# Two-layer kernel: layer one projected from the raw split input, recurrent and merge stages in one block

## The chip, the cores and the metric

One core of a Trainium2 chip runs one launch. The metric is the device time of the launch in microseconds (us). The engines are named TensorE (PE), VectorE (DVE), ScalarE (ACT), GpSimd (POOL) and SyncE (SP, which issues DMAs).

## The reference, cut to what matters

Two transformer layers over 512 tokens of width 1024 (16 meta tokens are put in front in layer one, so 528).

```python
# layer one
u = rmsnorm(h, norm_mix_pre); proj = u @ w_in         # q_na k_na v_na q_gl k_gl v_gl g_gl z_gl
o = concat(rmsnorm(neighbourhood_attention(...)), gla_bidirectional(...))
h = h + rmsnorm(o @ w_o, norm_mix_post)
h = h + rmsnorm((gelu(gate) * val) @ w_ffn_out, norm_ffn_post)   # gate, val: convolved h @ w_ffn_in
# layer two
proj = rms_norm(x, norm_mix) @ w_in
attn = windowed_gqa(q, k, v, sink)                    # 512 wide
rw = rwkv7_time_mix(zr, ...)                          # recurrent branch, 512 wide
merged = gates[0] * (attn @ w_up_attn) + gates[1] * (rw @ w_up_rwkv)
x = x + merged @ w_out
x = x + square(relu(rms_norm(x) @ w_ff1)) @ w_ff2
x = x + (p @ w_ple) * sigmoid(rms_norm(x) @ w_ple_gate)
```

The norm multiplies each token by a scalar: `(h * gain * rs) @ w` equals `((h * gain) @ w) * rs`, with `rs` one number per token.

## The kernel before

**Products.** Every large product is done in three passes (`three_pass`, L238): weights and input are each split into a high part (fp32r, written by ACT) and a low part (the rest, written by DVE), and hi·hi, lo·hi and hi·lo are summed in PSUM. Weights come in slots of 128 x 2048 through a ring of two places (`Ring`, L152). For each slot SP loads `raw` (L205), ACT writes `hi` (`hi_slot`, L215), DVE writes `lo` and raises `split` (`lo_slot`, L228), and PE raises `tile_done` per tile and waits for `tile_free` before it reuses a bank. Each engine works through its own list in order.

**Opening of the mixer (`mixer_block`).** SP loads h in four pieces, then the narrow slot (32 columns of z) and the two slots of `fm_gla` (L511 to L516). ACT squares h tile by tile (L292), PE sums the squares with a matrix of ones (L300), ACT takes the root (L884), DVE the reciprocal over all 528 tokens (L1078). DVE then writes `h * gain * rs` (L1084), ACT its high part `u_hi` (L889), DVE its low part `u_lo` (L1090). PE starts the first tiles (narrow slot and slot 1) k by k after `u_done`, then slot 2 (`fm_gla`'s second), which goes into the ring place that the narrow slot held. ACT evicts these tiles (L891, L898). The token-major slots (`tm_gla`, L589 to L593) follow. POOL issues 64 small loads of the bias rows from the beginning (L550).

**GLA stage.** While PE works through the gated recurrence (decays, scores, outputs for t = 0 to 4), the products of `fm_na` and `tm_na` are dealt into PE's order in counted portions (`run(name)`), 24 matmuls to a tile, two banks in turn. ACT evicts them in `evacuate` (L931 to L937) after its exponentials; DVE splits the next slot in `split_more`. The scores of the neighbourhood attention are scaled by 0.125 on DVE (L1254).

**Recurrent stage (`rwkv_block`).** Eight units (u = 0 to 7) with five levels each. Then the state loop: for 7 chunks and two directions, DVE multiplies by a decay (L2769), PE makes products (L2483), DVE adds them (L2767). Then y for four token tiles (PE L2498, DVE L2778 to L2786, ACT squares L2598), the normalisation (L2788, L2791), and for four fi: PE transposes and gate product (L2510, L2512), ACT scale (L2605), DVE bonus and gate (L2794, L2797, `rw_t`).

**Merge stage (`merge_block`).** It has its own block: the semaphores are cleared and all engines meet (L3161, L3162), the ring's weights are loaded anew. ACT and DVE split `attn_t` and `rw_t` (L2955, L3027), PE makes 16 tiles of the up-projection, 12 matmuls of 512 columns each: eight for the attention half, eight for the recurrent half. Per tile ACT opens a gate (sigmoid, L2962), DVE multiplies (L3037), and in the second half adds the two (L3040), ACT and DVE split the sum (L2965, L3048). Then come `w_out`, four groups of `w_ff1` and `w_ff2`, and the last gate.

## Time and profile before

| | us |
|---|---|
| median of 3 runs (1850.02 to 1853.32) | 1852.45 |
| the profiled execution | 1852.69 |
| its span in the profile | 1850.9 |
| mean granted clock of TensorE | 0.974 of full |

| engine | busy us | share of the span |
|---|---|---|
| PE (matmul) | 1729.4 | 93% |
| DVE | 1018.9 | 55% |
| ACT | 650.9 | 35% |
| POOL | 88.4 | 5% |

Rows of a timeline begin with start and duration; what ended an engine's idle time stands in brackets with the idle time. Granted clock 1.00 is 2.4 GHz, 0.50 is 1.2 GHz. A matmul on fp32 (not fp32r) data is recorded as two instructions.

### The profile page before, as it was taken

Reading aid. Unit: us, or ns where it says so; the run is one execution under the profiler, and the core shown is the slowest. Engines: PE = TensorE matmul, PEld = TensorE weight load, DVE = VectorE, ACT = ScalarE, POOL = GpSimd, SP = SyncE. Lnnn points to the kernel's source line nnn. Section 1 sums busy time; section 2 is a strip of 40 time slices with the busy share of each in tenths; the row PEclk is TensorE's granted clock in tenths of the full one; section 3 lists DMA queues with packets and bytes.
Section 4 is the critical chain, followed back from the end, with each engine's and each line's share of the span. In section 5 each row is a group of like instructions: output and inputs, shape, how many; then the busy total and the mean of one; then the engine's idle time right before and its main releaser. Section 6 shows DMA issues by size and latency. Waiting matters only on the chain. (4 is left out here: it accounts for less than half of the span.)

```text
span 1850.9 us, 38611 instructions
## 1 busy us (share of the span) xinstructions
PE 1729.4 (93%) x17168; PEld 1504.6 (81%) x17168; DVE 1018.9 (55%) x1527; ACT 650.9 (35%) x1067; POOL 88.4 (5%) x115
## 2 busy tenths in 40 slices
PE   6999999889999999899999988888499999999998
PEld 5899978889989989797777777777287888888887
DVE  3237776456726636538664465564656535353565
ACT  3243335434424323433443333332334312121332
POOL 7000000100000000100000000000002000000020
PEclk9999999989999999899999999999799999999999
DMA  5211120311232222222222100000142222222221
GB/s 169 92 69 46 70 94 10 109 53 69 91 114 92 92 91 92 98 81 80 92 100 77 41 4 4 4 4 10 66 180 87 99 104 92 93 99 105 91 92 68
DMA packets 29132, 144.57 MB, mean 78 GB/s; under 512 B 6315, under 2 KB 9659, under 8 KB 14380
## 3 DMA queue, kind: packets, MB, share of 16 engines
q1 hardware_dynamic: 24828, 133.58, 20.0%
q0 software_dynamic: 3856, 7.87, 1.5%
q8 instruction: 132, 2.16, 0.5%
q10 hardware_dynamic: 288, 0.73, 0.1%
q14 instruction: 28, 0.23, 0.0%
HBM read 134.82 MB, written 8.91 MB: 78 GB/s over the span
## 5 line engine op out<-in xcount | busy, mean ns | idle before, releaser
L228 DVE TENSOR_TENSOR w_w_lo<-w_w_raw,w_w_hi 128x2048 fp32r<-128x2048 f32 x66 | 151.2, 2291 | 178.5 <-ACT w_w_hi L215 178.1
L240 PE MATMUL f_bank<-u_hi,w_w_hi 128*128 128x258 f32 x704 | 202.4, 287 | 5.0 <-DVE u_lo L1486 4.2
L241 PE MATMUL f_bank<-u_hi,w_w_lo 128*128 128x258 f32 x704 | 201.3, 286 | 0.0
L242 PE MATMUL f_bank<-u_lo,w_w_hi 128*128 128x258 f32 x704 | 199.9, 284 | 0.0
L240 PE MATMUL g_bank<-g_y_hi,g_w_hi 128*128 128x512 f32 x384 | 151.1, 393 | 12.2 <-DVE g_w_lo L228 12.1
L241 PE MATMUL g_bank<-g_y_hi,g_w_lo 128*128 128x512 f32 x384 | 150.4, 392 | 0.0
L242 PE MATMUL g_bank<-g_y_lo,g_w_hi 128*128 128x512 f32 x384 | 150.4, 392 | 0.0
L215 ACT ACTIVATE g_w_hi<-g_w_raw 128x2048 fp32r<-128x2048 f32 x45 | 85.9, 1909 | 163.5 <-PE g_bank L242 161.9
L240 PEld LDWEIGHTS f_bank<-u_hi,w_w_hi 128*128 128x128 f32 x704 | 134.1, 191 | 5.6 <-issue 4.7
L215 ACT ACTIVATE w_w_hi<-w_w_raw 128x2048 fp32r<-128x2048 f32 x66 | 125.8, 1905 | 30.9 <-PE f_bank L242 30.9
L228 DVE TENSOR_TENSOR g_w_lo<-g_w_raw,g_w_hi 128x2048 fp32r<-128x2048 f32 x45 | 108.3, 2408 | 49.6 <-ACT g_w_hi L215 49.6
L242 PEld LDWEIGHTS f_bank<-u_lo,w_w_hi 128*128 128x128 f32 x704 | 135.1, 192 | 0.0
L241 PEld LDWEIGHTS f_bank<-u_hi,w_w_lo 128*128 128x128 f32 x704 | 134.5, 191 | 0.1
L240 PE MATMUL g_bank<-g_u_hi,g_w_hi 128*128 128x512 f32 x320 | 125.4, 392 | 2.6 <-DVE g_u_lo L3048 2.6
L241 PE MATMUL g_bank<-g_u_hi,g_w_lo 128*128 128x512 f32 x320 | 125.2, 391 | 0.0
L242 PE MATMUL g_bank<-g_u_lo,g_w_hi 128*128 128x512 f32 x320 | 125.0, 391 | 0.0
L1727 PE MATMUL a_bank<-u_hi,w_w_hi 128*128 128x512 f32 x240 | 98.6, 411 | 2.3 <-DVE shift L2047 1.6
L1731 PE MATMUL a_bank<-u_lo,w_w_hi 128*128 128x512 f32 x240 | 97.8, 407 | 0.0
L1729 PE MATMUL a_bank<-u_hi,w_w_lo 128*128 128x512 f32 x240 | 97.7, 407 | 0.0
L240 PEld LDWEIGHTS g_bank<-g_y_hi,g_w_hi 128*128 128x128 f32 x384 | 72.7, 189 | 28.5 <-issue 13.4
L242 PEld LDWEIGHTS g_bank<-g_y_lo,g_w_hi 128*128 128x128 f32 x384 | 72.7, 189 | 15.4
L241 PEld LDWEIGHTS g_bank<-g_y_hi,g_w_lo 128*128 128x128 f32 x384 | 72.8, 190 | 15.0
(510 smaller groups left out, 3904.6 us busy)
## 6 DMA issues: line engine op xcount, KB each, us to landing
g_w_raw<-in_w_ff SPq DMA_DIRECT2D x32, 1024.0 KB, 4.8
w_w_raw<-in_w_in SPq DMA_DIRECT2D x30, 1024.0 KB, 4.8
w_w_raw<-in_w_ffn_in SPq DMA_DIRECT2D x22, 1024.0 KB, 4.8
w_w_raw<-in_w_ffn_out SPq DMA_DIRECT2D x12, 1024.0 KB, 4.8
w_w_raw<-in_w_o SPq DMA_DIRECT2D x4, 1024.0 KB, 5.0
gate_pre<-rw_t POOLq DMA_DIRECT2D x16, 256.0 KB, 2.3
g_w_raw<-in_w_up SPq DMA_DIRECT2D x4, 1024.0 KB, 8.8
g_branch<-gate_pre SPq DMA_DIRECT2D x4, 1024.0 KB, 11.8
```

The source lines that it names most:

```text
L215: nc.scalar.activation(R.hi[:, r, 0:size], R.raw[:, r, 0:size], ACT.Copy).then_inc(R.hi_done, 1)
L228: nc.vector.tensor_tensor(R.lo[:, r, 0:size], R.raw[:, r, 0:size], R.hi[:, r, 0:size].bitcast(F32), ALU.subtract).then_inc(R.split, 1)
L240: nc.tensor.matmul(out, w_hi, u_hi, start=start, stop=False)
L241: nc.tensor.matmul(out, w_lo, u_hi, start=False, stop=False)
L242: return nc.tensor.matmul(out, w_hi, u_lo, start=False, stop=stop)
L1727: nc.tensor.matmul(tile_bank(g), w_hi, u_hi[:, k, :], start=k == 0, stop=False)
L1729: nc.tensor.matmul(tile_bank(g), w_lo, u_hi[:, k, :], start=False, stop=False)
L1731: last = nc.tensor.matmul(tile_bank(g), w_hi, u_lo[:, k, :], start=False, stop=k == KT - 1)
```

## The change

**Layer one.** The projection takes `h * gain` without the token's scalar. ACT writes its high part straight from h, DVE its low part, and slot 1 is loaded and split in two halves (`PART`), the narrow slot gets a place of its own. Squares go on alongside and are added by DVE; PE sums them after k = 4 into one column per token tile, and after k = 6 spreads the reciprocal roots to a row (`rms`). The scalar is applied at eviction: by DVE as a product with `rms` for the feature-major tiles (now also the first eight tiles of `fm_na`, which are the keys, loaded first), by ACT's scale for the token-major ones, and for the queries in the attention scores (`rs_query`). POOL's 64 bias loads wait for the narrow tile.

**Layer two.** The recurrent and merge stages share one block; POOL clears the attention stage's semaphores during the third unit and after it. The merge stage's buffers are placed over dead ones (`Merge`). During the last unit ACT and DVE split `attn_t` and slot 0 of `w_up`. PE's attention half of the up-projection (96 matmuls) is dealt into the state loop (12), before y of the last tile (7), after it (50), and into the loop over fi (0, 6, 3, 18). ACT copies those tiles out, POOL splits slots 1 and 2 and multiplies the attention half by its gates, ACT and DVE split `rw_t` per fi. Gates are loaded after y. The merge stage keeps only slots 2 and 3.

```diff
+            sp.dma_start(R.raw[:, 1, 0:PART], w[4, :, 0:PART]).then_inc(part_loaded, 16)
+            load_h(0)
             sp.dma_start(narrow(R.raw[:, 0, :]), narrow(w[12, :, :])).then_inc(R.loaded[0], 16)
-            load_phase(sp, R, fm_gla, w[4:6])
+            load_h(1)
+            sp.dma_start(R.raw[:, 1, PART:2 * PART], w[4, :, PART:2 * PART]).then_inc(R.loaded[1], 16)
+            load_h(2)
+            load_h(3)
+            sp.wait_ge(R.split, 1)
+            sp.dma_start(R.raw[:, 0, :], w[5, :, :]).then_inc(R.loaded[0], 16)
-            load_phase(sp, R, fm_na, w[0:4])
+            load_phase(sp, R, fm_na, w[0:4], at=(2, 3, 0, 1))
...
+            pool.wait_ge(R.tile_done, zz.end())
...
+                if k == 4:
+                    pe.wait_ge(const_loaded, 16)
+                    pe.wait_ge(added, KT - 1)
+                    for t in range(5):
+                        last = nc.tensor.matmul(bank[0:size[t], 6, t:t + 1], sq_all[:, tok[t]], C("ones")[:, 0:1], start=True, stop=True)
...
+            scaled_hi(1)
+            scaled_hi(2)
+            act.wait_ge(R.loaded[1], 16)
+            nc.scalar.activation(R.hi[:, 1, PART:2 * PART], R.raw[:, 1, PART:2 * PART], ACT.Copy).then_inc(R.hi_done, 1)
+            square(0)
+            square(1)
+            for k in range(3, KT):
+                scaled_hi(k)
+                square(k - 1)
+            square(KT - 1)
...
+            for k in range(3, KT):
+                scaled_lo(k)
+                add_square(k - 1)
+            add_square(KT - 1)
...
+                    dve.wait_ge(R.tile_done, fm_gla.c0 + 2 * j + m + 1)
+                    nc.vector.tensor_tensor(gla_in[:, 2 * j + m, :].rearrange("p (a b) -> p a b", a=2), bank[:, b:b + 2, 0:HALF], row,
+                                            ALU.mult).then_inc(R.tile_free, 1)
...
+        @block.gpsimd
+        def _(pool):
+            def low(n):
+                pool.wait_ge(M.R.hi_done, n + 1)
+                nc.gpsimd.tensor_tensor(M.R.lo[:, n % 2, :], M.R.raw[:, n % 2, :], M.R.hi[:, n % 2, :].bitcast(F32), ALU.subtract).then_inc(M.R.split, 1)
+
+            pool.wait_ge(d_done, NU)
+            low(1)
+            low(2)
+            for t in range(KT):
+                pool.wait_ge(M.R.tile_free, t + 1)
+                pool.wait_ge(M.gate_open_a, t + 1)
+                nc.gpsimd.tensor_tensor(M.branch[:, t, :], M.branch[:, t, :], M.gate[:, t, :], ALU.mult).then_inc(M.gated, 1)
...
                     last.then_inc(step_done, 1)
+                    run_attn(1)
...
+                if t == 3:
+                    run_attn(7)
...
                 last.then_inc(y_done, 1)
+            run_attn(50)
...
                 nc.tensor.matmul(bank[:, fi % 2, :], lora_g[:, fi * P:fi * P + P], zr[:, 13, :], start=True, stop=True).then_inc(gl_done, 1)
+                run_attn((0, 6, 3, 18)[fi])
...
+            act.wait_ge(rp_read, NU)
+            hi_slot(act, nc, M.R, 0, 1, None)
+            keep_attn(0)
...
+            keep_attn(3)
+            hi_slot(act, nc, M.R, 1, 0, 4)
+            keep_attn(4)
...
+                if fi == 0:
+                    keep_attn(5)
+                else:
+                    split_branch(fi - 1)
+                open_gate(fi)
...
-            each_slot(dve, up, up_slot)
+            dve.wait_ge(R.split, 3)
+            for j in (2, 3):
+                up_slot(j, 1, j % 2)
...
-        nc.clear_and_free_semaphores(nc.allocated_since(before))
-        nc.all_engine_barrier()
...
-        merge_block(nc, io, C, PV, h, attn_t, rw_t, gate_pre)
+            merge_block(nc, io, C, PV, h, M, w.sem["rw_done"], block)
```

## Rows read from the trace of the kernel before

**Rows 1.** The page, busy time of TensorE.

```profile
PE 1729.4 (93%) x17168; PEld 1504.6 (81%) x17168; DVE 1018.9 (55%) x1527; ACT 650.9 (35%) x1067; POOL 88.4 (5%) x115
```

**Rows 2.** Stretches: us, busy PE, PEld, DVE, ACT, POOL (instructions), clock, DMA, GB/s.

```profile
3.00:4.50 1.50, 0.00 (x0) 0.00 (x0) 0.00 (x0) 0.00 (x0) 1.50 (x4) 1.00 0.96 383
...
18.90:27.70 8.80, 0.00 (x0) 0.00 (x0) 7.76 (x6) 4.00 (x5) 8.80 (x18) 0.78 0.74 173
...
30.40:44.00 13.60, 13.60 (x113) 13.15 (x113) 6.83 (x11) 2.71 (x5) 4.51 (x9) 0.99 0.20 49
```

**Rows 3.** Timeline of PE in the opening.

```profile
27.77 0.40 PE L240 MATMUL m_bank<-u_hi,w_w_hi 128*32 128x264 f32 x1 [8.89 <-DVE u_lo L1090]
...
50.05 0.39 PE L240 MATMUL m_bank<-u_hi,w_w_hi 128*128 128x264 f32 x1 [3.37 <-DVE w_w_lo L228]
...
64.25 0.36 PE L589 MATMUL m_bank<-w_w_hi,u_hi 128*128 128x256 f32 x1 [0.79 <-ACT m_gla_in L898]
```

**Rows 4.** Timeline of DVE and ACT in the opening.

```profile
19.86 3.45 DVE L1078 RECIPROCAL m_work<-m_work 128x528 f32<-128x528 f32 x1 [1.42 <-ACT m_work L884]
...
24.16 0.64 ACT L889 ACTIVATE u_hi<-m_work 128x528 fp32r<-128x528 f32 x1 [2.52 <-DVE m_work L1084]
...
26.92 0.70 DVE L1090 TENSOR_TENSOR u_lo<-m_work,u_hi 128x528 fp32r<-128x528 f32 x1
...
45.77 1.90 ACT L215 ACTIVATE w_w_hi<-w_w_raw 128x2048 fp32r<-128x2048 f32 x1
```

**Rows 5.** The tile h in the opening: time from issue to landing.

```profile
DMA to landing us min/median/max: 5.6/8.2/10.1
```

**Rows 6.** Timeline of ACT and DVE in the GLA stage, t = 1.

```profile
145.61 0.60 ACT L949 ACTIVATE m_work<-m_bank 128x512 f32<-128x512 f32 x1 [2.35 <-PE m_bank L663]
...
147.64 0.41 ACT L932 ACTIVATE acc<-m_bank 128x256 f32<-128x256 f32 x1
...
150.91 2.29 DVE L228 TENSOR_TENSOR w_w_lo<-w_w_raw,w_w_hi 128x2048 fp32r<-128x2048 f32 x1 [1.45 <-ACT w_w_hi L215]
```

**Rows 7.** Stretches of the tail and of the feed-forward part.

```profile
1312.00:1320.00 8.00, 0.00 (x0) 0.00 (x0) 5.55 (x12) 2.77 (x4) 0.00 (x0) 0.50 0.00 0
...
1333.00:1342.40 9.40, 0.00 (x0) 0.00 (x0) 6.79 (x3) 7.44 (x4) 0.00 (x0) 0.58 0.85 336
...
1400.00:1600.00 200.00, 200.00 (x896) 166.01 (x895) 99.15 (x98) 54.97 (x53) 13.75 (x7) 1.00 0.28 99
```

**Rows 8.** Timelines of DVE, PE and ACT in the tail.

```profile
1292.30 0.42 DVE L2769 TENSOR_TENSOR r_s<-r_s,small 128x256 f32<-128x256 f32 x1
...
1294.45 1.48 PE L2483 MATMUL r_bank<-r_s,r_gi 64*64 64x64 f32 x32 [0.19 <-DVE r_s L2769]
...
1319.64 2.50 DVE L2791 TENSOR_TENSOR zr<-zr,r_stat 128x512 f32<-128x512 f32 x4
...
1331.05 0.69 DVE L2797 TENSOR_TENSOR rw_t<-r_bank,acc 128x512 f32<-128x512 f32 x1
...
1342.50 1.28 ACT L2962 ACT_TABLE_LOAD   x1
1343.80 2.19 ACT L2962 ACTIVATE g_branch<-g_branch 128x512 f32<-128x512 f32 x4
...
1371.43 0.68 DVE L3037 TENSOR_TENSOR g_branch<-g_bank,g_branch 128x512 f32<-128x512 f32 x1
```

**Rows 9.** Chain of waits where the output projection starts: start, us, what.

```profile
1395.86 0.75 PE g_bank L240
1396.61 0.43 PE g_bank L241
```

**Rows 10.** Timelines of DVE and POOL where both work.

```profile
1418.75 3.38 DVE L228 TENSOR_TENSOR g_w_lo<-g_w_raw,g_w_hi 128x2048 fp32r<-128x2048 f32 x1
...
1418.65 4.64 POOL L310 TENSOR_TENSOR g_rows<-g_rows,g_branch 128x512 f32<-128x512 f32 x2 [6.93 <-ACT g_branch L2932]
...
747.93 1.09 POOL L310 TENSOR_TENSOR f_a<-f_a,f_c 128x512 f32<-128x512 f32 x1
```

More of the change, by code:

```diff
@@ L596, in token_tile @@
                     yield
+            pe.wait_ge(row_steps, TURNED)
+            for c in range(NB):
+                last = nc.tensor.matmul(bank[:, 6, 128 + c:129 + c], by_column[:, P * c:P * c + P], eye[:, 0:1], start=True, stop=True)
+            last.then_inc(row_steps, 1)
             def raw(t):
@@ L2198, in __init__, with __getitem__ @@
         self.half_w0, self.half_a0 = small[:, at:at + 2 * RW_FI], small[:, at + 2 * RW_FI:at + 4 * RW_FI]
-def rwkv_block(nc, io, C, PV, w, block, before):
+class Halves:
+    def __init__(self, first, second):
+        self.parts = (first, second)
+    def __getitem__(self, key):
+        rows, i, cols = key
+        half = (i.start if isinstance(i, slice) else i) // KT
+        i = slice(i.start - KT * half, i.stop - KT * half) if isinstance(i, slice) else i - KT * half
+        return self.parts[half][rows, i, cols]
```

485 lines of the change are left out of this document (343 added, 142 removed).

## The prediction

> **What bounds the kernel now.** I read the page's busy times first, then tables of stretches, then the timelines of the two places that the diff touches. TensorE (PE) is busy 93% of the span [rows 1], so an edit pays where PE stands still or runs at half clock. PE has two such places here.
>
> The opening: PE runs the norm's sums early, does nothing from 18.9 to 27.7 us, restarts at half clock, and then turns out a projection matmul of 264 columns every 0.120 us (13.60 us for 113) [rows 2]. The first starts at 27.77, released by the scaled and split activations; slot 2 starts at 50.05 after 3.37 us of waiting for its low half; the token-major slots start at 64.25, 0.79 us after an eviction by ACT [rows 3]. Behind 27.77 stands a serial chain: squares, sums, root, a 3.45 us reciprocal, scaling, splitting [rows 4].
>
> The tail: PE has no instruction from 1312 to 1320 (clock at 1.2 GHz, 0.50) and from 1333 to 1342.4, while the feed-forward part is full at 0.223 us a matmul of 512 columns (200 us for 896) [rows 7]. The last rw_t is written at 1331.05 to 1331.74, two semaphore and load steps follow, and the up-projection's 192 matmuls all come after that [rows 8]. The chain of waits enters the output projection at 1395.86 at half clock (0.75 for the first) [rows 9].
>
> **Opening, part by part.** Removed from PE's path: the 16 norm sums, root, reciprocal over 528 columns, normalising pass, and slot 2's dependence on the narrow slot's place. Added before PE: half a slot split (ACT 0.95, DVE 1.15, half of 1.90 and 2.29 [rows 4, 6]), one scaled copy (0.64) and one low half (0.70) [rows 4]. The loads are reordered; the POOL's 64 bias loads go behind the first tile. The first pieces: half of w4 (0.5 MB), h0 (0.54 MB) and params. DMA gives 383 GB/s when loaded [rows 2]; h landed 5.6 us after issue at best, 10.1 at worst [rows 5]. Half a slot ahead of h0 adds 0.5 MB / 383 GB/s = 1.4 us, less what consts takes now: h0 at about 7.2. Then the 0.64 and 0.70 and their waits make u 0 at 8.8, with weights split by 8.1. PE starts at 8.8.
>
> From there the DVE sets the pace: up to the second half slot, landing at about 11.2 and split at 13.4, it has little to do; then five pairs of low half and addition, 1.35 each, and two single additions: sum of squares ready at 21.5. PE has then done five of eight k (18 matmuls each, 2.16: 8.8 to 19.6 at full clock, 21 if it starts at half), waits to 21.5, and has three k (6.5), five sums and five spreads left (1.2 together): 29.2. Root, small reciprocals and diagonals (about 2.3 after the sums) lie under k = 5 and 6. Slot 2 is loaded by 17, split by 26.8, its bank freed by a DVE product of 0.7 to 0.8 under k = 7. Its 96 matmuls take 11.7: 40.9; one eviction by DVE, four small query sums in parallel, 0.8: token-major slots start at 41.7 in place of 64.25, **minus 22.5**. Ends: minus 24 (PE begins at 8, full clock) and minus 18 (h2 and h3 land 4 us later than 14).
>
> **Evictions moved to DVE.** Eight key half-tiles go from ACT to DVE inside the GLA stage, where PE is full. In step t = 1 ACT evicts a tile at 147.64, but DVE finishes its own products only at 149.46 (150.91 less 1.45). PE takes up the fill at 145.6, when ACT is released, and after 26 matmuls of 0.115, at 148.6, needs that bank: 24 matmuls make a tile, and there are two banks [rows 6]. The DVE then evicts in 0.6, in the 1.45 us it idles before the weight split [rows 6]: PE loses 1.4 here and 1.0 by the same reckoning in t = 2: **plus 2.4**; 0 if ACT's exponentials shift, 4 if t = 0 joins. Scales by a column in place of a constant: nothing, same instructions.
>
> **Tail, part by part.** All in the old times.
> (a) Unit 7 takes eight half-microsecond ACT pieces and eight DVE pieces of 0.6 into idle time of over 2 us a level: 0.
> (b) The state loop has a period of 1.67 us, DVE's four operations of 0.42, and PE waits only 0.19 of it [rows 8]. Two fill matmuls of 0.22 do not fit: (2 x 0.22 - 0.19) x 6 = **plus 1.6** (0 to 2.8, all twelve).
> (c) POOL now splits slot 1 as soon as ACT's high half is done, about 1292.2, just when DVE multiplies states (both inputs in SBUF). Where the two meet in the trace, a DVE split of 2.29 took 3.38, and two POOL additions of 1.09 took 4.64 [rows 6, 10]: they exclude each other for an instruction's length. POOL at 1.09 per 512 columns needs at least 4.4 for 2048. **Plus 4.4** (0 if the operation falls between, 5.2).
> (d) The y stage is DVE's; PE fills there, so it keeps its clock. From yn at 1322.14 [rows 8], ACT gets between its four scalings one kept tile, a table load of 1.28, four sigmoids at 0.55 [rows 8] and three splits: it becomes the limit. Step by step: rw_t 3 at 1333.9 and its split at 1335.1, **2.2 later** than now. POOL's second split and its first four gate products meet bonus and low-half operations of DVE: **plus 2.5** (0 to 4.8, four products of 1.2).
> (e) PE's last 18 fill matmuls end at 1335.6. The eight recurrent tiles take 96 x 0.227 = 21.8: 1357.4. The barrier, the attention half, four loads and the first weight split are gone from the path.
> (f) DVE then has multiply, add, low half per tile (0.7 + 0.6 + 0.6 [rows 8]), plus two weight splits of 2.3, and ends at 1362.6; three matmuls of the last k close output tile 0 at 1363.3. Now it ends at 1395.86 + 6 x 0.43 = 1398.4.
> Sum of the tail: 1363.3 + 1.6 + 4.4 + 2.5 = 1371.8, so **minus 26.6**. Ends: minus 35.1 (none of the pluses) and minus 20 (all upper ends, and 1.2 for POOL under slot 3's split).
>
> On the trace's 3.38 for 2.29: the Trainium skill, SBUF — State Buffer, section "Who interferes with whom", says that a DVE instruction with two SBUF inputs and a GpSimd instruction that reads SBUF cannot run together, and the later one waits for the whole of the other. The trace agrees [rows 10]; by the rule the tail has its 6.9 us of (c) and (d), and if the two engines shared instead it would have none of them, which is rival 1.
>
> **Sum.** Against the profiled execution's 1852.69 (span 1850.9, 1.8 around it; the median of the runs, 1852.45, is the same within 0.02%): 1852.7 - 22.5 + 2.4 - 26.6 = **1806.0**.
>
> **Rivals.**
> 1. *POOL and DVE miss each other*: POOL works when DVE reads PSUM (adds, y sums). Against it: half the state loop's DVE time reads SBUF twice [rows 8]. 1806.0 - 6.9 = 1799.1.
> 2. *The loads set the opening*: h3, last in the queue, lands 4 us later; DMA stands at 383 GB/s in the early stretch [rows 2], and the whole of 4 MB must pass. For it: h0 alone took 5.6. Against: the bias loads are out of the way. 1806.0 + 4.5 = 1810.5.
> 3. *The fill is not hidden*: PE has its attention matmuls in order before work that the recurrence needs; if all 96 (21.8 us) lie on the path in place of 1.6, 1806.0 + 20.2 = 1826.2. Against: PE stood idle or at half clock from 1312 to 1320 [rows 7].
> 4. *Slower than before*: POOL's split of slot 1. PE's fill tile 4 waits for it ahead of the gate transposes, at about 1316; begun at 1292, it has 24 us. Beyond, each microsecond counts in full, and 24 + 46.7 = 71 us for 2048 columns (18 us per 512) is where the change begins to lose; at 80 us it gives 1862. The rows show 1.09 to 2.8 per 512 columns, so this would need a different kind of operation.
> 5. *The change doesn't do it*: something (a wait on the cleared semaphores in unit 7, a gate load) holds the merge stage to its old start, and only the opening is won: 1852.7 - 20.1 = 1832.6.
>
> **How the numbers follow.** Forecast case 61% (1800 to 1812 on its own terms), rival 1 15%, rival 2 11%, rival 3 5%, rival 4 4% (a quarter of it near its turning point), rival 5 4%. The range 1794 to 1819 runs from all lower ends (1852.7 - 24 - 35.1 = 1793.6) to all upper ends (1852.7 - 18 + 4 - 20 = 1818.7), and leaves out rivals 3 to 5, 13%, and some of the forecast case's tails. A measurement of this kernel can tell about 0.2%, 3.7 us. Faster by more 96%, within it 1%, slower 3%.
>
> **What would show it.** Right: PE's first matmul near 9 us with a wait of some 2 us before the sums; the first token-major matmul near 42; a DVE state product of 4 to 5 us beside a POOL operation of as much; PE filled from 1290 to 1322 (old times); recurrent tiles starting 13.5 us after yn; GLA 2 us longer. Wrong: a POOL split that takes 8 us or more, state products untouched, PE waiting at the second half slot, or a DVE chain after the last recurrent tile of over 5 us.

## The result, and the profile after

| | before | after |
|---|---|---|
| median, us | 1852.88 (4 runs, 1850.02 to 1854.08) | 1822.49 (4 runs, 1816.23 to 1830.32) |
| profiled execution / its span, us | 1852.69 / 1850.9 | 1830.32 / 1828.5 |
| ratio, 95% interval | | 0.9843, 0.9817 to 0.9869 |

The change makes the kernel 30 us faster; 47 were forecast. The forecast was 1806.0 us, its range 1794 to 1819: the time lies outside. The profiled execution is the slowest of the four, 7.8 us above their median, so what is laid out below accounts for a gain of 22.4 us and not of 30. Two executions that had a mean granted clock of 0.84, one of an experiment (1931.87 us) and one of the kernel before (1966.58 us), are left out of the comparisons.

Where the two profiles part is found by laying DVE's instructions, which are nearly the same in both, side by side. Offset is after less before, at the same instruction:

| DVE instruction | before | after | offset | my sum there |
|---|---|---|---|---|
| weight split L228, start of the token-major slots | 65.94 | 47.13 | -18.8 | -22.5 |
| copy to m_state, inside the GLA stage | 168.91 | 153.04 | -15.9 | -20.1 |
| copy to the selector, start of the units | 1058.72 | 1043.39 | -15.3 | -20.1 |
| first sum behind unit 7 | 1287.80 | 1275.71 | -12.1 | -20.1 |
| first addition behind the state loop | 1303.51 | 1305.68 | +2.2 | -14.1 |
| last rw_t | 1331.05 | 1337.22 | +6.2 | -9.4 |
| first addition of the output projection | 1404.58 | 1373.21 | -31.4 | -46.7 |
| last product but one of the kernel | 1845.68 | 1823.31 | -22.4 | -46.7 |

Four places take back what was forecast: the opening (3.7 us), the units (3.2), the state loop (14.3 in place of 6.0) and, largest and not in the forecast at all, the feed-forward part (9.0). The step that replaces the merge stage's start by dealt fill gave 37.6 us (6.2 + 31.4) where the sum has 37.3.

Page of the changed kernel: busy times, and the granted clock in tenths over 40 slices.

```profile
PE 1738.0 (95%) x17164; PEld 1502.6 (82%) x17164; DVE 1023.2 (56%) x1546; ACT 653.7 (36%) x1073; POOL 110.7 (6%) x125
...
PEclk9999999989999999899999999999799999999999
...
q8 instruction: 132, 2.16, 0.5%
```

PE is busier than before [rows 1], in a shorter span: fewer holes, but slower matmuls. The 7 in the clock row is the state loop. The queue of instructions (packets, MB, share) comes up again in the units.

Timeline of ACT and PE in the opening of the changed kernel:

```profile
8.46 0.73 ACT L916 ACTIVATE u_hi<-h,params 128x528 fp32r<-128x528 f32 x1 [1.61 <-DMA h<-in_h]
...
10.14 0.56 PE L240 MATMUL m_bank<-u_hi,w_w_hi 128*128 128x264 f32 x1 [10.14 <-DVE u_lo L1132]
...
15.12 0.42 PE L241 MATMUL m_bank<-u_hi,w_w_lo 128*128 128x264 f32 x1
15.34 0.34 PE L242 MATMUL m_bank<-u_lo,w_w_hi 128*128 128x264 f32 x1
15.52 0.28 PE L240 MATMUL m_bank<-u_hi,w_w_hi 128*128 128x264 f32 x1
...
44.13 0.95 PE L627 MATMUL m_bank<-consts,m_work 128*128 128x1 f32 x8
45.44 0.36 PE L616 MATMUL m_bank<-w_w_hi,u_hi 128*128 128x256 f32 x1 [0.36 <-ACT m_st L950]
```

ACT's first scaled copy waits for the first piece of h, which was issued at 1.20 and landed 7.2 us later. PE starts at 10.14 in place of 27.77 [rows 3], runs its first matmuls 0.22 us apart, that is at half clock, until 15.3, then 0.12 apart, and never waits before 45.

Stretches around the state loop, changed kernel (us, busy PE, PEld, DVE, ACT, POOL with instructions, clock, DMA share, GB/s), and the loop's stretch of the kernel before:

```profile
1266.00:1279.40 13.40, 9.30 (x367) 8.32 (x358) 7.66 (x15) 5.21 (x9) 0.00 (x0) 1.00 0.23 82
1279.40:1292.00 12.60, 9.72 (x97) 6.64 (x96) 7.34 (x12) 0.60 (x1) 4.51 (x1) 0.59 0.24 85
1292.00:1305.00 13.00, 12.73 (x148) 9.25 (x149) 5.46 (x13) 0.60 (x1) 0.00 (x0) 0.50 0.00 1
```

```profile
1287.00:1303.00 16.00, 11.92 (x378) 10.20 (x371) 12.25 (x29) 0.60 (x1) 0.00 (x0) 1.00 0.01 3
```

The same loop ran at 1.00 before and runs at 0.50 to 0.59 now. Its timeline in the changed kernel (PE, POOL and DVE; L3058 is the addition that closes each half step, L3060 the state product):

```profile
1278.80 0.35 PE L2694 MATMUL r_bank<-r_s,r_gi 64*64 64x64 f32 x5 [1.26 <-DVE r_s L3060]
1280.14 4.51 POOL L2456 TENSOR_TENSOR g_lo<-g_raw,g_hi 128x2048 fp32r<-128x2048 f32 x1 [236.91 <-ACT g_hi L215]
1280.76 0.56 PE L2694 MATMUL r_bank<-r_s,r_gi 64*64 64x64 f32 x11 [1.60 <-issue]
1281.36 0.42 DVE L3058 TENSOR_TENSOR r_s<-r_bank,r_s 128x256 f32<-128x256 f32 x1 [2.37 <-PE r_bank L2694]
1281.82 3.12 DVE L3060 TENSOR_TENSOR r_s<-r_s,small 128x256 f32<-128x256 f32 x1
1284.86 0.41 DVE L3058 TENSOR_TENSOR r_s<-r_bank,r_s 128x256 f32<-128x256 f32 x1
...
1293.25 0.42 DVE L3058 TENSOR_TENSOR r_s<-r_bank,r_s 128x256 f32<-128x256 f32 x1 [0.89 <-PE r_bank L2694]
1295.02 0.42 DVE L3058 TENSOR_TENSOR r_s<-r_bank,r_s 128x256 f32<-128x256 f32 x1 [0.89 <-PE r_bank L2694]
```

Three things are to be seen. PE stands for 1.60 us in the middle of a step with its data there (issue). A state product of 0.42 us takes 3.12 beside POOL's split. And each half step takes 1.77 us (1293.25 to 1295.02), of which DVE now waits 0.89 for PE; before, it was half of 1.67. Laid beside the kernel before, the 14.3 us of this stage come to 1.6 up to the first addition (the stop), 2.7 in the half step with POOL, 8.9 in the ten half steps behind it, and 1.0 on the way to y's first addition.

Feed-forward part, 200 us of the changed kernel and of the kernel before (us, busy PE with the count of matmuls, clock, DMA share, GB/s):

```profile
1500.00:1700.00 200.00, 200.00 (x865) 1.00 0.27 95
```

```profile
1500.00:1700.00 200.00, 200.00 (x884) 1.00 0.27 100
```

Both are full and at clock 1.00, and yet the changed kernel puts through 865 matmuls where the other has 884: 0.231 us each against 0.226. Over the 446 us from 1404.58 to the end, 2.2% is 9.8 us; the offsets give 9.0.

### The profile page after: what moved, and what is told of

Its sections match the earlier page's. It is cut to its first block, busy times and chain, and to the rows that moved or that the text cites. A ratio compares the mean times of both kernels' runs of the same rounds, so it can differ in the third digit from the quotient of the medians.

```text
span 1828.5 us, 38642 instructions
## 1 busy us (share of the span) xinstructions
PE 1738.0 (95%) x17164; PEld 1502.6 (82%) x17164; DVE 1023.2 (56%) x1546; ACT 653.7 (36%) x1073; POOL 110.7 (6%) x125
## 3 DMA queue, kind: packets, MB, share of 16 engines
q1 hardware_dynamic: 24972, 133.58, 20.5%
## 4 chain that ended last, share of the span: by engine, by line
PE 79%; DVE 6%; ACT 3%; issue 3%; POOL 0%; DVEq 0%; ACTq 0%; POOLq 0%
PE g_bank L240 8%; PE g_bank L242 8%; PE g_bank L241 8%; PE f_bank L240 7%; PE f_bank L241 7%; PE f_bank L242 7%; PE r_bank L2543 4%; PE a_bank L1820 3%; PE a_bank L1824 3%; PE a_bank L1822 2%; PE m_bank L667 1%; PE m_bank L795 1%; PE r_bank L2516 1%; PE a_bank L1883 1%; PE m_bank L855 1%
## 5 line engine op out<-in xcount | busy, mean ns | idle before, releaser
L228 DVE TENSOR_TENSOR w_w_lo<-w_w_raw,w_w_hi 128x2048 fp32r<-128x2048 f32 x65 | 148.9, 2291 | 157.5 <-ACT w_w_hi L215 157.1
L241 PE MATMUL g_bank<-g_y_hi,g_lo 128*128 128x512 f32 x352 | 139.4, 396 | 0.0
L242 PE MATMUL g_bank<-g_y_lo,g_hi 128*128 128x512 f32 x352 | 139.2, 395 | 0.0
L240 PE MATMUL g_bank<-g_y_hi,g_hi 128*128 128x512 f32 x352 | 138.4, 393 | 0.0
L215 ACT ACTIVATE g_hi<-g_raw 128x2048 fp32r<-128x2048 f32 x44 | 84.0, 1908 | 146.3 <-PE g_bank L242 146.3
L228 DVE TENSOR_TENSOR g_lo<-g_raw,g_hi 128x2048 fp32r<-128x2048 f32 x42 | 101.8, 2424 | 51.0 <-ACT g_hi L215 51.0
L240 PE MATMUL g_bank<-g_u_hi,g_hi 128*128 128x512 f32 x320 | 126.0, 394 | 0.2 <-DVE g_u_lo L3329 0.2
L242 PE MATMUL g_bank<-g_u_lo,g_hi 128*128 128x512 f32 x320 | 125.6, 392 | 0.0
L241 PE MATMUL g_bank<-g_u_hi,g_lo 128*128 128x512 f32 x320 | 125.0, 391 | 0.0
L240 PEld LDWEIGHTS g_bank<-g_y_hi,g_hi 128*128 128x128 f32 x352 | 66.1, 188 | 16.3 <-issue 0.4
L241 PEld LDWEIGHTS g_bank<-g_y_hi,g_lo 128*128 128x128 f32 x352 | 66.0, 187 | 16.1
```

Of the source, the lines that this page charges most:

```text
L215: nc.scalar.activation(R.hi[:, r, 0:size], R.raw[:, r, 0:size], ACT.Copy).then_inc(R.hi_done, 1)
L228: nc.vector.tensor_tensor(R.lo[:, r, 0:size], R.raw[:, r, 0:size], R.hi[:, r, 0:size].bitcast(F32), ALU.subtract).then_inc(R.split, 1)
L240: nc.tensor.matmul(out, w_hi, u_hi, start=start, stop=False)
L241: nc.tensor.matmul(out, w_lo, u_hi, start=False, stop=False)
L242: return nc.tensor.matmul(out, w_hi, u_lo, start=False, stop=stop)
```

## Experiments

Ratios are to the kernel before, on the same chip; "the changed kernel" is after.

### The change again, and its two halves

**After, once more.** No edit.

> The changed kernel once more, unaltered, beside the others. What is asked is what repeats. Theory A (the gain is lost at places that belong to the kernel): the granted clock again falls to 0.5 to 0.6 somewhere in the state loop (0.57 and 0.51 in two stretches of some 12 us of the first profile), the state loop again ends about 14 us later against the kernel before than it began, and in the feed-forward part a matmul of 512 columns again follows the last by 0.231 us, where the kernel before has 0.227: 1822 us, ratio 0.984. Theory B (that profile was unlucky): the stretches of the state loop stay at 1.00 and the pitch is 0.227, and the time is 1822.5 less 8 for the loop and less 8.8 for the feed-forward part, about 1806.

1825.27 us, ratio 0.9839 (0.9811 to 0.9868). Both places repeat in its profile: the state loop again moves the offset by 14.3 us, from -14.3 to 0.0, at half clock, and the feed-forward part from -33.6 to -24.8. Theory A: these two losses belong to the kernel. The units do not repeat: they lose 1.3 us here where they lost 3.2.

**The opening alone.** The mixer block and its loads are the changed ones, the tail is the old one.

> The kernel before with the new opening alone: the mixer block and its loads are those of the change, the recurrent and the merge stage are two blocks as before. From the profiles of the two kernels, after the opening and the GLA stage the changed one is 15.9 us ahead and stays so until the recurrent units begin. Theory A (the edits are independent): 1852.7 - 15.9 = 1836.8, ratio 0.9914, with the feed-forward part at a pitch of 0.227 us and the state loop at a granted clock of 1.00. Theory B (what the opening changes reaches to the end, for instance by the clock that is granted later): the feed-forward part drifts by the 8.8 us that the changed kernel shows, 1845.6, ratio 0.996.

1828.60 us, ratio 0.9865 (0.9846 to 0.9884): 24.5 us, 9 more than expected and 4 more than my sum has for opening and evictions together (20.1). Its state loop is at clock 1.00 with half steps of 0.80 and 0.87 us, and its feed-forward part has 884 matmuls in 200 us: neither loss comes from the opening. Theory B is out; theory A has the places right and the size wrong. Part of the rest is the clock in layer one, which goes its own way. Changed kernel, then this one, where layer one's feed-forward part ends and layer two begins:

```profile
750.00:790.00 40.00, 35.20 (x210) 0.74 0.18 60
```

```profile
750.00:790.00 40.00, 35.20 (x247) 0.83 0.21 74
```

A stretch at 0.83 against 0.74 lets 37 more matmuls through in the same busy time. At this place the offset to the kernel before goes to -20.5 here and stays at -15.3 in the changed kernel. Two kernels below with the same code up to the state loop (the combined ones) differ in the same way, 0.74 and 0.83, so which of the two it is belongs to the execution. It may need the new opening all the same: the half clock at this place lasts 13.7 us in place of 20.5 in eight of the twelve profiles with the new opening and in none of the six with the old one. Whether that is the opening's doing, no run here shows. Executions of the changed kernel lie 14 and 10 us apart in its two sets of four (6 us for this kernel), and this is at least a part of it; it limits what medians can tell. Profiles tell more.

**The tail alone.** Changed kernel with the old mixer block.

> The changed kernel with the old opening (the mixer block and its loads of the kernel before): the tail's change alone. Theory A (independent edits): the whole gain of the changed kernel, 30.2 us, less the 15.9 of the opening and the GLA stage is 14.3: 1852.7 - 14.3 = 1838.4, ratio 0.9923, with the half clock in the state loop and a pitch of 0.231 us in the feed-forward part, as these come from the tail's own edits. Theory B (the half clock in the state loop depends on what came long before): no such stretch here, and 8 us less, 1830, ratio 0.988. Theory C (my forecast of the tail, 26.6 us): 1826.1.

1844.51 us, ratio 0.9954 (0.9937 to 0.9971): 8.7 us and not 14 or more. The profile has all the tail's losses: offset 0 to +5.2 over the units, +17.7 behind the loop (half clock from its start, a product of 3.29 us beside POOL), and -15.8 to -6.8 over the feed-forward part. Theory A holds for places, though its time was 6 us too low; B and C are out. So the forecast fails in the tail: 26.6 us forecast, 8.7 measured. The two halves alone add up to 33 us, the whole change gave 30.

### The feed-forward part

In the kernel before, weights, u and y stand one behind the other, and all their addresses leave the same remainder, 288, when divided by 512 bytes. In the changed kernel they are placed over dead buffers: the high parts of the weights, the low part of slot 1 and y_lo still leave 288, but the low part of slot 0, y_hi and u_lo leave 480, and u_hi 32.

**Only the places.** The kernel before, its merge buffers at the changed kernel's addresses.

```diff
-        R = Ring(ctx, nc, "g")
+        R.hi = Pair(place("hi0", slot, acc_at, F32R), place("hi1", slot, r_at, F32R))
+        R.lo = Pair(place("lo0", slot, q_at, F32R), place("lo1", slot, r_at + size_, F32R))
...
+        u_hi, u_lo = place("u_hi", [P, KT, GRID], spare_at + 2 * size_, F32R), place("u_lo", [P, KT, GRID], rw_at, F32R)
```

> The kernel before, with the merge stage's buffers (weight slots, splits, branch, y, u, gates' rows) at the SBUF places that they have in the changed kernel, scattered in place of one after the other; nothing else differs. Theory A (places set the pace of the feed-forward part's matmuls): its pitch goes from 0.227 to 0.231 us and the time to 1852.7 + 8.8 = 1861.5, ratio 1.0047. Theory B (places are indifferent; the pitch comes from the instruction stream of one block, or from the run): within 0.1% of the kernel before, ratio 1.000.

1861.11 us, ratio 1.0044 (1.0031 to 1.0057): +8.0, with nothing else changed. Theory A.

```profile
1500.00:1700.00 200.00, 200.00 (x866) 1.00 0.27 95
```

**The order kept, 192 bytes left free** behind the weight slots of the kernel before.

```diff
         R = Ring(ctx, nc, "g")
+        sb("shift_by", [P, 48])
```

> The kernel before, with 192 bytes a partition left free in the merge stage between the weight slots and the activations, branches and rows. The buffers stay one behind the other; only the remainder of the activations' addresses by 512 bytes changes against that of the weights (from 0 to 192). Theory A (the pitch depends on that remainder, as the changed kernel's buffers have it, 192 or 256 between u or y and the weights): a matmul of 512 columns follows the last by 0.230 to 0.236 us in place of 0.2267, and over the 1950 matmuls of this stage the time rises by 6 to 18 us: 1859 to 1871, ratio 1.004 to 1.010. Theory B (scattering is what counts, far-apart buffers or other regions): unchanged, ratio 1.000.

1864.48 us, ratio 1.0057 (1.0037 to 1.0078), 859 matmuls in the 200 us. No buffer was scattered; the remainder is enough.

```profile
1500.00:1700.00 200.00, 200.00 (x859) 1.00 0.26 94
```

**512 bytes, and 64 bytes**, in the same place (`[P, 128]`, `[P, 16]`).

> The kernel before with 512 bytes a partition left free between the weight slots and the activations of the merge stage (192 bytes made it 9 us slower, pitch 0.231 to 0.232 us in place of 0.2267). Theory A (only the remainder by 512 counts): the pitch is 0.2267 us again and the ratio 1.000. Theory B (any displacement breaks the regular row of buffers): as with 192 bytes, ratio 1.005.

> The kernel before with 64 bytes left free in the same place. Theory A (every remainder but 0 costs, about the same): pitch 0.231 us, ratio 1.005. Theory B (the cost grows with the remainder): a third of that of 192 bytes or less, ratio 1.001 to 1.002. Theory C (only displacement in larger steps counts): 1.000.

With 512 bytes 1852.84 us, ratio 1.0005 (0.9992 to 1.0019); with 64 bytes 1857.07 us, ratio 1.0016 (1.0001 to 1.0031). First 512, then 64:

```profile
1500.00:1700.00 200.00, 200.00 (x884) 1.00 0.28 98
```

```profile
1500.00:1700.00 200.00, 200.00 (x876) 1.00 0.28 95
```

884 matmuls with 0 or 512 bytes, 876 with 64, 859 with 192: the remainder counts, not the displacement, and of the two shifts that cost something the larger costs more (theories A for 512 and B for 64).

**The cure on the changed kernel.** All operands of TensorE at one remainder.

```diff
+                ctx.enter_context(nc.sbuf_tensor("shift_by", [P, 48], F32, side="right"))
                 attn_t, rw_t = (ctx.enter_context(nc.sbuf_tensor(n, [P, 4, GRID], F32, side="right")) for n in ("attn_t", "rw_t"))
...
-        spare_at = gi_at + 36 * 1024 + 1024 // 4
+        spare_at = gi_at + 36 * 1024 + 512
```

> The changed kernel, with its merge stage's buffers moved by 192 bytes downwards (those on the right side) or 256 upwards (loads and u), so that all that TensorE reads in the feed-forward part stands at the same remainder by 512 bytes; their order and regions stay. Theory A (remainder): the pitch falls from 0.231 to 0.2267 us, and the time from 1825 by 8.8 us to 1816, ratio 0.979. Theory B (regions or distance): the pitch stays at 0.231 us and the time at 1825, ratio 0.984.

1811.75 us, ratio 0.9775 (0.9754 to 0.9796), theory A. The offset to the kernel before is -42.9 at the output projection's first addition, and the spans differ by 42.8: the drift of 9 us is gone. That the median lies 4 us below theory A's time is not the edit's: in this profile the half clock at the state loop lasts 6.8 us in place of 23.9.

```profile
1500.00:1700.00 200.00, 200.00 (x884) 1.00 0.28 99
```

One thing is not separated. In every kernel at full pace all operands leave 288, so the runs do not tell whether the difference between weights and activations counts or the remainder of each by itself, nor whether it is TensorE's own reads that are slowed or their meeting with those of ACT and DVE.

### The state loop

**POOL out of the loop.**

```diff
             pool.wait_ge(d_done, NU)
+            pool.wait_ge(state_done, 2 * (NCH - 1))
             low(1)
```

> The changed kernel, with one wait added: POOL begins its split of weight slot 1 only when the DVE has done all its state products, so that in the state loop nothing of POOL reads SBUF. Theory A (the DVE is held up by POOL there, my term c): one state product or addition of over 3 us is gone, the loop gets 4 us shorter, and the granted clock stays as it is; about 1821, ratio to the kernel before 0.982. Theory B (the loop is slow because TensorE runs at half clock in it and stands on the loop's path with its recurrence products and one fill matmul a half step, 1.05 + 0.72 us): the split of POOL lay beside that, the half step stays at 1.77 us, and the time stays at 1825, ratio 0.984.

1822.07 us, ratio 0.9823 (0.9792 to 0.9855). Timeline of DVE, the additions (L3059) and a product:

```profile
1276.30 0.42 DVE L3059 TENSOR_TENSOR r_s<-r_bank,r_s 128x256 f32<-128x256 f32 x1 [2.37 <-PE r_bank L2695]
1276.76 0.42 DVE L3061 TENSOR_TENSOR r_s<-r_s,small 128x256 f32<-128x256 f32 x1
1277.88 0.42 DVE L3059 TENSOR_TENSOR r_s<-r_bank,r_s 128x256 f32<-128x256 f32 x1 [0.70 <-PE r_bank L2695]
1279.66 0.42 DVE L3059 TENSOR_TENSOR r_s<-r_bank,r_s 128x256 f32<-128x256 f32 x1 [0.89 <-PE r_bank L2695]
...
1287.79 0.42 DVE L3059 TENSOR_TENSOR r_s<-r_bank,r_s 128x256 f32<-128x256 f32 x1 [0.16 <-PE r_bank L2695]
1288.83 0.42 DVE L3059 TENSOR_TENSOR r_s<-r_bank,r_s 128x256 f32<-128x256 f32 x1 [0.15 <-PE r_bank L2695]
```

The product is back at 0.42, and the first interval falls from 3.50 to 1.58 us: POOL's price is 1.9, not the 4.4 of my term (c). The rest stays, as theory B has it, and this loop happens to see both clocks: a half step takes 1.77 us (1277.88 to 1279.66) while the clock is 0.5, and 1.04 (1287.79 to 1288.83) when it is back. Each theory is right about its part; the median cannot tell them apart.

**The fill out of the loop**, behind it (`run_attn(12)` ahead of the y stage in place of `run_attn(1)` in each half step).

> The changed kernel, with the twelve attention matmuls taken out of the state loop and put right behind it; nothing else differs. In the profiles of the changed kernel the loop takes 28 us, in those of the kernel before 14. Theory A (the fill makes the loop's path longer at half clock): without it the half step falls from 1.77 to 1.05 + 0.3 = 1.35 us at half clock, or to 0.83 at full clock; over the 12 to 14 half steps 5 to 12 us less, against which the twelve matmuls stand behind it, where TensorE has room: 1825 - 5 to 12 = 1813 to 1820, ratio 0.978 to 0.982. Theory B (the clock falls by itself after unit 7, and the loop is as long as the clock is low): half the loss stays. Theory C (the fill is what keeps the clock from being low for longer): the clock is at 0.5 through the y stage too, as in the kernel before from 1310 to 1327, and the time rises to 1830.

1817.27 us, ratio 0.9795 (0.9776 to 0.9815): 5 to 8 us better than the changed kernel. Not all of the difference between the profiles is the edit's: this one is 21.3 us ahead of the kernel before where the units begin, the changed kernel's was 15.3. The state loop itself takes back 7.5 us here in place of 14.3. Timeline of DVE:

```profile
1280.15 0.42 DVE L3058 TENSOR_TENSOR r_s<-r_bank,r_s 128x256 f32<-128x256 f32 x1 [0.43 <-PE r_bank L2694]
1281.00 0.42 DVE L3058 TENSOR_TENSOR r_s<-r_bank,r_s 128x256 f32<-128x256 f32 x1
1282.25 0.42 DVE L3058 TENSOR_TENSOR r_s<-r_bank,r_s 128x256 f32<-128x256 f32 x1 [0.37 <-PE r_bank L2694]
1283.11 0.42 DVE L3058 TENSOR_TENSOR r_s<-r_bank,r_s 128x256 f32<-128x256 f32 x1
...
1287.66 0.42 DVE L3058 TENSOR_TENSOR r_s<-r_bank,r_s 128x256 f32<-128x256 f32 x1
1288.46 0.42 DVE L3058 TENSOR_TENSOR r_s<-r_bank,r_s 128x256 f32<-128x256 f32 x1
```

Without fill two half steps take 2.10 us at half clock (1280.15 to 1282.25), 1.05 each, and 0.83 at full. So one fill matmul a half step costs 0.2 us at full clock and 0.7 at half. Theory A for the size (6.8 us in the loop); the clock fell all the same at the loop's start, as B says, and came back on its own, against C.

**The fill ahead of the loop**, where PE stands (with the buffers at one remainder).

```diff
+            run_attn(12)
             pe.wait_ge(y0_read, NU)
...
-                    run_attn(1)
```

> The changed kernel with the merge buffers at one remainder (1811.8 us, ratio 0.9775 by itself), and the twelve attention matmuls taken out of the state loop and put ahead of it, where TensorE stands: 1.25 us for the DVE's first product, then 5 matmuls, then another 1.6 us without an instruction, after which the granted clock falls to 0.5. Theory A (the clock falls because TensorE stands there): with 2.7 us of full matmuls in that place it stays at 1.00 through the loop, the half step is 0.83 us throughout, the 1.6 us gap shrinks, and 7 to 9 us are won: 1803 to 1805, ratio 0.973. Theory B (the clock falls whatever stands there, for what the units did before): only the fill's own cost in the loop goes (0.21 us a half step at full clock, 0.7 at half), 2 to 4 us: 1808 to 1810, ratio 0.9755.

1804.19 us, ratio 0.9749 (0.9720 to 0.9777). Its stretches before and in the loop:

```profile
1264.00:1276.00 12.00, 9.14 (x262) 1.00 0.24 90
1276.00:1288.00 12.00, 8.23 (x196) 1.00 0.25 90
```

The loop runs at 1.00 throughout, in half steps of 0.83 us but for the first, and takes back 4.3 us in place of 14.3: theory A, on one execution, which a second one below bears out and a third does not. One thing in it was wrong: the stop for no visible reason did not shrink (1.69 us), it only stands among full matmuls now. In all nine profiles with the changed tail and the fill in the loop or behind it the clock fell at the loop's start, and PE had just stood there for 1.25 us for the DVE's first product and for another 0.9 to 1.9 us of issue before or after it. The kernel before has the 1.25 us alone (1289.62 to 1290.87), and its clock holds.

**Remainder and fill behind the loop together.**

> The two edits together that each won by themselves: merge buffers at one remainder (10 to 13 us over the changed kernel) and the twelve fill matmuls behind the state loop (5 to 8 us). They touch different stages, so the sum should hold: 1811.8 less about 5 = 1807, ratio 0.975, with the clock still falling for 7 to 10 us at the loop's start, and the pitch in the feed-forward part at 0.2267 us.

1807.12 us (three executions, 1804.90 to 1813.06), ratio 0.9772 (0.9743 to 0.9800). The profile has what was expected (a half clock of some 7 us at the loop's start, 0.226 us a matmul). The median is the 1807 of the forecast, the ratio that of the remainder alone (0.9775): three executions that lie 8 us apart do not settle whether the 5 us add. In the profiles the loop takes back 7.1 us here and 8.1 with the remainder alone.

**What the loop takes back, profile by profile** (by how much the offset moves between the first sum behind unit 7 and y's first addition, and how long the stretch of half clock is that begins at the loop; the last two edits are described further down):

| kernel | us taken back | us at half clock |
|---|---|---|
| changed; once more; tail alone | 14.3; 14.3; 12.5 | 23.9; 27.3; 20.5 |
| POOL out of the loop; fill behind it | 8.1; 7.5 | 10.2; 10.2 |
| remainder; remainder and fill behind | 8.1; 7.1 | 6.8; 6.8 |
| remainder and second load later; remainder and warm start | 14.2; 14.6 | 23.9; 23.9 |
| remainder and fill ahead | 4.3 | none |

The changed kernel, the tail alone, the remainder, the second load later and the warm start have the same instructions in the loop, fill and POOL included, and take back between 8.1 and 14.6 us, by how long the half clock lasts. No edit of these sets that length, and it is worth as much as POOL or the fill. Only with the fill ahead of the loop did the half clock not come.

### The units, and the opening

The recurrent units lose 1 to 5 us in the kernels with the changed tail (3.2 and 1.3 in the two profiles of the changed kernel, 5.1 with the tail alone, 3.7 with one remainder). The waits of PE over them, first in the kernel before, then in the changed kernel with one remainder (us in total, times, longest):

```profile
PE r_bank L2360 <- issue: 11.7, 19, 1.4
```

```profile
PE r_bank L2543 <- issue: 11.8, 16, 2.7
```

The longest stop, 2.7 us at 1137, comes just behind two weight loads of 1 MB that the changed kernel issues there. But the two sums are alike, though the second profile's units are 3.7 us longer. What differs besides is the clock over the units, first before, then with one remainder (us, busy PE, clock, DMA share, GB/s):

```profile
1058.70:1287.80 229.10, 192.75 (x7312) 0.99 0.03 6
```

```profile
1037.70:1270.40 232.70, 195.72 (x7310) 0.97 0.05 16
```

It is at 0.50 for 3.4 us before and for 13.7 us, in four short stretches, here; one of them begins at 1137.6, at the end of that stop. In the profile with POOL out of the loop it is the other way round: the clock is at 1.00 over the whole units, and they lose 4.9 us all the same. So the loss has two parts, whose shares change from one execution to the next.

**The second load later.**

```diff
             load_up(0)
+            sp.wait_ge(tt_done, 4 * (NU - 2))
             load_up(1)
```

> The merge buffers at one remainder, and of the two weight loads of 1 MB that stand one right behind the other in the recurrent units (274 GB/s at about 1135 us) the second is issued only near unit 6. Where they stand now, TensorE has its longest stop without a cause that the profile shows: 2.5 to 2.7 us, where the kernel before has stops of 0.9 there; its instructions come as packets of 16 KB about every 4 us on the same DMA engines. Theory A (the loads delay the instruction packets): the stop is 1.0 to 1.7 us, a second one of that size appears where the load went, and the sum over the units is about the same or up to 1 us less: 1811. Theory B (the stop has nothing to do with the loads): it stays at over 2.5 us at its place.

1812.53 us, ratio 0.9778 (0.9756 to 0.9799), no gain in the median. PE's stop there is 0.98, the longest anywhere 1.7:

```profile
PE r_bank L2544 <- issue: 11.1, 15, 1.7
```

and a new one of 1.13 stands where the load went. The stop at this place lasts 2.5 to 4.7 us in the nine profiles with both loads together, and 1.0 to 1.6 in the three with the second one later. The units lose 1.3 us in this profile. Theory A: loads delay TensorE, possibly by way of its instructions, which come through a DMA queue of their own, 132 packets of 16 KB in the page's row; that link is argued from the coincidence and not shown. The loop of this execution was at half clock for its whole length, which hides the little that was won.

**A warm start**: four matmuls on zeros from 1.5 us on, thrown away, while PE waits.

```diff
+            pe.wait_ge(cleared, 1)
+            for _ in range(4):
+                nc.tensor.matmul(bank[:, 6, :], vg[:, 4, 0:P], vg[:, 4, 0:512], start=True, stop=True)
             pe.wait_ge(part_split, 2)
```

> The merge buffers at one remainder, and four matmuls of 512 columns on a buffer of zeros (their result is thrown away) that TensorE runs from about 1.7 us on, while it waits for the first weights. In the changed kernel its first matmuls, from 10.14 to 15.3 us, follow each other by 0.22 us, half clock, and then by 0.12. Theory A (the start at half clock is what is missing of my 22.5 us, besides 1.3 us of a later landing): the first matmuls follow by 0.12 us from the start or from 12 us on; TensorE then waits for the DVE or the sum of squares at some point, so 1 to 2.3 us are won: 1810, ratio 0.9765. Theory B (loads or the DVE set the pace in any case): the opening ends as before, 1811.8.

1812.84 us, ratio 0.9777 (0.9754 to 0.9800). PE's timeline:

```profile
1.47 6.73 PE L579 MATMUL m_bank<-m_vg 128*128 128x512 f32 x8 [1.47 <-DVE m_vg L1129]
10.15 0.36 PE L240 MATMUL m_bank<-u_hi,w_w_hi 128*128 128x264 f32 x1 [1.96 <-DVE u_lo L1135]
10.35 0.29 PE L241 MATMUL m_bank<-u_hi,w_w_lo 128*128 128x264 f32 x1
...
11.13 0.42 PE L241 MATMUL m_bank<-u_hi,w_w_lo 128*128 128x264 f32 x1
11.35 0.42 PE L242 MATMUL m_bank<-u_lo,w_w_hi 128*128 128x264 f32 x1
```

It starts at full clock, but PE stood for 1.96 us before, and at 11.0 the clock falls after all, until 14.4. The token-major slots start at 44.59, where the changed kernel has 45.44, the remainder alone 45.12 and the kernel with POOL out of the loop, whose opening is the same, 44.73. What is won is not clear of this scatter, and the median is that of the remainder alone: theory B fits better.

**All together**, with six matmuls on zeros, and the same with POOL's wait.

> The changed kernel with four edits: merge buffers at one remainder, the twelve fill matmuls ahead of the state loop, the second weight load near unit 6, and six matmuls on zeros at the start (four ended at 8.2 us, TensorE stood for 1.96 us, and the clock fell at 11.0 for 3.4 us; six should reach to 9.9). Theory A (drops of the clock follow stops of TensorE, and each edit removes one): against the first two alone (1804) 2 us in the opening and 2 to 3 in the units: 1799, ratio 0.972. Theory B (what is won in one place moves the drop to another): 1804, ratio 0.975.

> The same four edits, and POOL's split of slot 1 waits for the end of the state loop. Theory A (the DVE waits for POOL in the loop): the first half steps take 0.83 in place of 1.74 us, 1 to 2 us less: 1798, ratio 0.971. Theory B (POOL then holds the DVE up in the y stage that follows, as a 1.5 us statistics step showed when this wait was added to the changed kernel): no gain, 1799.

1806.75 us, ratio 0.9758 (0.9737 to 0.9780), and 1804.89 us, ratio 0.9756 (0.9728 to 0.9784). Neither beats remainder and fill ahead (1804.19), from which they cannot be told apart. In the first the six matmuls ran until 9.8, PE stood for 0.33 us, and the clock held at the start but fell at 24.5 for 3.4 us; the token-major slots start at 45.87, later than without the warm start. In the second they ended at 8.3, since the later ones ran at full clock, PE stood for 1.84 us, and the clock fell at 11.2 as with four. In the first a stop of 3.33 us came ahead of the loop and the clock fell there in spite of the fill, twice for 3.4 us; in the second it did not fall, and no POOL is in the loop:

```profile
1275.80 0.42 DVE L3063 TENSOR_TENSOR r_s<-r_bank,r_s 128x256 f32<-128x256 f32 x1 [2.22 <-PE r_bank L2700]
1276.60 0.42 DVE L3063 TENSOR_TENSOR r_s<-r_bank,r_s 128x256 f32<-128x256 f32 x1
1277.46 0.42 DVE L3063 TENSOR_TENSOR r_s<-r_bank,r_s 128x256 f32<-128x256 f32 x1
```

Half steps of 0.80 and 0.86 from the first on: the loop as it was before the change. In the execution of the remainder-and-fill kernel the first took 1.74, so POOL costs 0.9 us there. For the medians theory B holds: what is won in one place is within what the clock takes elsewhere.

## Why the prediction was wrong, point by point

Two steps failed most, both in the tail. The feed-forward part stood at nothing, because its instructions are the same, and measured 9.0 us. The state loop, (b) and (c), stood at 6.0 us, priced at full clock, and measured 14.3 with the clock at half.

**Opening, -22.5 forecast, -18.8.** The step "PE starts at 8.8" was 1.3 us early, because "h0 at about 7.2" was: the first piece of h landed 7.2 us after its issue at 1.20, so ACT could begin at 8.46. The scaled copy (0.73) and the low half (0.77) took the 1.6 us of the sum within 0.1. The step that failed by more is "waits to 21.5": I let the start at half clock vanish in that wait. There was none: PE was itself the late one, the fifth k ended at 23.5, 2.0 us after the wait I had. The later start is 1.3 us of that, and the 23 matmuls at 0.22 in place of 0.12 cost 2.3 us where I had 1.4. The sums and spreads took 2.3 us where I had 1.2 (1.1 more), and query sums and ACT's copy, 44.13 to 45.44, took 1.3 where I had 0.8. Slot 2's 96 matmuls took the 11.7 of the sum. Run alone, opening and evictions gave 24.5 us in the median where the sum has 20.1, so it is not here that the forecast was lost.

**Evictions, +2.4.** Measured +2.9 by the offsets, 0.9 in t = 1 and 1.9 in t = 2 where I had 1.4 and 1.0, and +2.8 in the profile of the opening alone. Right, with the two parts the other way round.

**(a) Unit 7 takes its pieces for nothing.** The units lost 3.2 us, and between 0.9 and 5.1 in the other kernels with this tail. I priced the instructions that were added and neither the 2 MB of loads, beside which PE stood for 2.5 us, nor the clock, which was at 0.50 for 6.8 us of the units in place of 3.4. That the added pieces themselves cost nothing is not shown by a run of its own.

**(b) and (c), +6.0 for the state loop; measured +14.3.** The step that failed is the loop's clock. The fill was priced at full clock only (1.6, though (2 x 0.22 - 0.19) x 6 is 1.5; at full clock it measures 12 x 0.2 = 2.5). At half clock it is 12 x 0.7, and the half step without fill also grows, from 0.83 to 1.05. I read the loop's clock, 1.00, from the trace before and kept it; yet the claim that fill "keeps its clock" stood for the y stage only, and there it holds (0.98 from 1305 to 1320, where it was 0.50 [rows 7]). (c) was too high: 4.4 for 1.9 (2.7 in the half step itself, of which some comes back in the next), since the DVE loses only what is left of POOL's instruction when it wants to read, and at half clock it has slack. Then 1.6 for a stop of PE.

**(d), +4.7; measured +4.0.** Right: DVE's first bonus product took 3.32 us beside POOL's second split and the next 1.28 beside a gate product, where they take 0.69 and 0.68 alone.

**(e) and (f), the merge stage's start: -37.3; measured -37.6.** The largest term of the change, and right within 1%.

**Feed-forward part, 0; measured +9.0.** Not a step of the sum at all. I took the stage as untouched since its instructions are; its addresses are not. Together with the opening's 3.7, the units' 3.2 and the loop's 8.3 this makes 24.2; the other terms add 0.1 between them, and that is the distance from 46.7 to the 22.4 us by which the two profiles differ. The median of the four executions is 16.5 us above the forecast; the 7.8 us between it and the profiled one are the execution's and not a step's. The 0.223 us of my second reading divides 200 us by 896 instructions, among them 24 small ones for the statistics; the sum itself used 0.227.

**The rivals.** 1 (POOL and DVE miss each other) is out: 3.12 and 3.29 us for a product of 0.42. 2 (the loads set the opening) gives its 4.5 us nearly by size. The start itself did wait for the first piece of h, 1.3 us longer than I had; after it PE never waited for a load. 3 (fill not hidden) is in the right place: the fill lies on the path in the loop, for 2.5 to 8 us (twelve times 0.2 or 0.7) and not for 20. Its time, 1826.2, is nearest of all, mostly for reasons of its neighbours. The rule that I cited from the Trainium skill, SBUF — State Buffer, section "Who interferes with whom", agrees with the runs: beside POOL's split of 4.51 us the DVE's product takes 3.12, without it 0.42. But whole instructions excluded means the remainder of the running one, not its full length added.

## What to carry to other kernels

When buffers are moved, compare the pitch of one full stretch of matmuls before and after, and keep all operands of TensorE at one remainder by 512 bytes, as they were here before the move (288): two lines took away a drift of 9 us in 1822. Work dealt into a loop whose matmuls are small has two prices, one at each clock; put it into the hole ahead of the loop, not between its steps; here the clock then held through the loop in two profiles of three. Price a step moved into a stage by its loads as well as by its instructions.

## What the hardware showed that was not expected

- Matmuls of 512 columns from 0.226 us each (200 us by their count) to 0.228, 0.231 and 0.233, by the remainder of the addresses alone, activations against weights (0; 64; mixed 192, 256 and 0; 192 bytes). Why is not known from these runs. The Trainium skill, TensorE: Matmul & The Clock Gate, section "Step-by-step: what each phase is for", says that TensorE reads weights and moving operand through two independent ports, and that loading weights takes nothing from the running matmul; by that a weight load would not slow the matmul beside it, wherever the two stand, and the section says nothing of addresses. The runs show that the addresses matter; they do not show whether the weight loads have a part in it.
- The granted clock fell within about a microsecond of a stop of PE of over 1 us between stretches of small matmuls, and stayed low for between 7 and 27 us in nine profiles (24 and 27 in the two of one program). It did not fall in the two profiles where a stop of 1.45 or 1.69 us had full matmuls ahead of it, nor in the kernel before, with a stop of 1.25; with the same matmuls and a stop of 3.33 it did, for 3.4 us. What decides the length is open.
- PE stood without a cause in the profile for 2.5 to 4.7 us behind the issue of 2 MB of loads (nine profiles), and for 1.0 to 1.6 when the second MB came later (three).
- A DVE product of 0.42 us took 3.12 beside a POOL split of 4.51 that had begun 1.7 us earlier, and 1.36 in the kernel with fill ahead.
